# A two-layer transformer in float32: narrow matmuls in the feed-forwards, and a second copy of the last activations

## The reference

```python
def swiglu(x, w_gate, w_up, w_down):
    return (jax.nn.silu(x @ w_gate) * (x @ w_up)) @ w_down

for layer in range(2):
    ...
    h = h + 0.5 * swiglu(rms_norm(h, ffn1_norm_g[layer]), ffn1_w_gate[layer], ffn1_w_up[layer], ffn1_w_down[layer])
    ...  # layer 0: gated convolution, layer 1: attention; both with attention to a memory, then w_o
    h = h + 0.5 * swiglu(rms_norm(h, ffn2_norm_g[layer]), ffn2_w_gate[layer], ffn2_w_up[layer], ffn2_w_down[layer])
# second block: one normed input times w_in_2 (queries, keys, values, gates), a differential
# attention and an mLSTM attention, gated sums, w_out_2, norm, added to x
```

## Time and profile before

| | |
|---|---|
| time, median of 3 runs | 1188.84 us (1188.67 to 1189.12) |
| the profiled execution | 1188.1 us, span of the core 1186.5 us |
| TensorE busy | 1179.0 us, 99% of the span |
| VectorE busy | 862.4 us, 73% |
| ScalarE busy | 677.9 us, 57% |
| granted TensorE clock, mean | 0.999 |
| DMA | 215.85 MB, 182 GB/s |

### The profile page before, as it was taken

One profiled execution on the slowest core, in us unless ns is written; L12 is line 12 of the kernel. 1 busy time (PEld: TensorE's weight loads), 2 busy tenths in 40 slices (PEclk: granted clock), 3 DMA queues, 4 the chain that ended last, 5 costly groups with the idle time before them and its releaser, 6 DMA issues.

```text
span 1186.5 us, 18987 instructions
## 1 busy us (share of the span) xinstructions
PE 1179.0 (99%) x7592; PEld 1044.4 (88%) x7592; DVE 862.4 (73%) x1213; ACT 677.9 (57%) x1036; POOL 68.5 (6%) x86
## 2 busy tenths in 40 slices
PE   9999999999999999999999999999999999999998
PEld 8888889969988888888888888998888899879996
DVE  7977766896887767787766677677776668666875
ACT  7766644546665545655544557566554545566463
POOL 1601000200010000000000022000000000000000
PEclk9999999999999999999999999999999999999999
DMA  8855656564655555546555553255555565536440
GB/s 308 302 195 179 194 177 204 201 178 136 203 192 181 187 184 193 199 173 208 192 173 181 174 190 129 72 196 189 195 185 178 193 204 190 180 127 196 138 165 35
DMA packets 65398, 215.85 MB, mean 182 GB/s; under 512 B 8352, under 2 KB 12064, under 8 KB 65184
## 3 DMA queue, kind: packets, MB, share of 16 engines
q1 hardware_dynamic: 62608, 210.64, 53.0%
q10 hardware_dynamic: 2704, 4.02, 1.0%
HBM read 212.70 MB, written 1.93 MB: 181 GB/s over the span
## 4 chain that ended last, share of the span: by engine, by line
PE 95%; DVE 2%; ACT 1%; DMA 1%; issue 1%; POOL 0%; SPq 0%; ACTq 0%; DVEq 0%; POOLq 0%
PE psum L509 93%; DMA raw<-in_slots 1%; DVE wlo L1864 1%; ACT whi L1253 0%; PE psum L920 0%; DVE small L2308 0%; DVE oa L2516 0%; DVE acc L1926 0%; PE psum L1062 0%; PE psum L880 0%; PE psum L673 0%; PE psum L1203 0%; PE psum L970 0%; PE psum L1011 0%; POOL small L2739 0%
## 5 line engine op out<-in xcount | busy, mean ns | idle before, releaser
L509 PE MATMUL psum<-x,whi 128*128 128x512 f32 (+1 forms) x2512 | 633.0, 343 | 0.4 <-DVE aq L2451 0.3
L1864 DVE TENSOR_TENSOR wlo<-raw,whi 128x1024 fp32r<-128x1024 f32 (+2 forms) x402 | 474.6, 1192 | 166.0 <-ACT whi L1253 163.4
L1253 ACT CAST whi<-raw 128x1024 fp32r<-128x1024 f32 (+2 forms) x402 | 405.2, 1021 | 155.6 <-PE psum L509 146.7
L509 PE MATMUL psum<-x,wlo 128*128 128x256 f32 x1960 | 430.5, 279 | 0.0
L509 PEld LDWEIGHTS psum<-x,wlo 128*128 128x128 f32 x1960 | 366.8, 188 | 57.8
L509 PEld LDWEIGHTS psum<-x,whi 128*128 128x128 f32 x2512 | 382.1, 188 | 2.5 <-issue 0.9
L509 PE MATMUL psum<-g,whi 128*128 128x512 f32 x704 | 218.7, 392 | 0.0
L509 PEld LDWEIGHTS psum<-g,wlo 128*128 128x128 f32 x704 | 132.2, 188 | 29.5
L509 PE MATMUL psum<-whi,x 128*128 128x512 f32 (+1 forms) x512 | 140.6, 375 | 0.0
L509 PE MATMUL psum<-g,wlo 128*128 128x256 f32 x704 | 139.1, 279 | 0.0
L509 PEld LDWEIGHTS psum<-g,whi 128*128 128x128 f32 x704 | 106.8, 188 | 0.0
(11 more groups left out here) (317 smaller groups left out, 796.4 us busy)
## 6 DMA issues: line engine op xcount, KB each, us to landing
raw<-in_slots SPq DMA_DIRECT2D x371, 512.0 KB, 4.1
raw<-in_slots SPq DMA_DIRECT2D x16, 384.0 KB, 3.3
raw<-in_slots SPq DMA_DIRECT2D x16, 256.0 KB, 2.6
h<-conv_mem SPq DMA_DIRECT2D x8, 284.0 KB, 4.9
mkv<-in_mem ACTq DMA_DIRECT2D x1, 1024.0 KB, 11.2
memt<-in_mem_cols ACTq DMA_DIRECT2D x1, 1024.0 KB, 14.5
conv_mem<-hc SPq DMA_DIRECT2D x3, 288.0 KB, 2.3
h<-conv_mem SPq DMA_DIRECT2D x4, 142.0 KB, 2.9
```

Of the source, the lines that this page charges most:

```text
L509: return pe.matmul(o, l, r, start=start, stop=stop, skip_group_check=True)
L1253: act.copy(held(B.whi[:, i % SPLIT, :], *n), held(B.raw[:, i % RAW, :], *n)).then_inc(*s.hi.now(i))
L1864: dve.tensor_tensor(held(B.wlo[:, i % SPLIT, :], *n), held(B.raw[:, i % RAW, :], *n), held(B.whi[:, i % SPLIT, :], *n).bitcast(F32), ALU.s ...
```

## The change

- Up and gate sums of most column pairs are made narrow: pairs 2 to 6 in the first feed-forward, 2 to 4 and 6 to 10 in the second, 2 to 10 in the third and fourth (`NARROW_UP`). Narrow pairs alternate between banks 0 and 1 (gate) and 2 and 3 (up), and VectorE scales and multiplies straight from PSUM; copy and addition of halves go.
- All down sums are made narrow, also without halves.
- In the second to fourth feed-forward, in a wide pair that a narrow one follows, the last slot of up changes its order: its third and fourth block issue their four rounded matmuls, then their four rest matmuls (`last`).
- The last feed-forward's `prep` writes a second copy of the next activations, into `rh[1]`, `rl[1]` (`w2r`), and the rows of the last stage read that one.

```diff
+NARROW_UP = (tuple(range(2, 7)), (2, 3, 4, 6, 7, 8, 9, 10), tuple(range(2, 11)), tuple(range(2, 11)))
...
-            if late:
+            if late or (last and i >= 2):
                 two_rounded(b, h[:, k, :], x[:, kc], start and i == 0)
...
         if late:
             pe.wait_ge(*s.lo.at(slot))
-            for kc in ks:
+        if late or last:
+            for kc in ks if late else ks[2:]:
                 t = two_left(b, l[:, kc % 4, :], x[:, kc], stop and kc == ks[-1])
...
+    def read(done, part, f, p, narrow):
+        if p - 1 not in NARROW_UP[f]:
+            pe.wait_ge(*s.sum.at((part, f, p - 1)))
+        elif not narrow:
+            pe.wait_ge(*done.at((f, p - 1)))
+        elif p - 2 in NARROW_UP[f]:
+            pe.wait_ge(*done.at((f, p - 2)))
...
+            if narrow:
+                pair(xi, 0, up_slot(f, p), gate, range(4), True, False)
+                pair(xi, 0, up_slot(f, p) + 1, gate, range(4, 8), False, True)
+                read(s.mul, "up", f, p, narrow)
+                pair(xi, 0, up_slot(f, p) + 2, up, range(4), True, False)
+                pair(xi, 0, up_slot(f, p) + 3, up, range(4, 8), False, True)
+            elif p:
+                cols(x, 8, up_slot(f, p), gate)
+                read(s.mul, "up", f, p, narrow)
+                cols(x, 8, up_slot(f, p) + 2, up, last=f > 0 and p + 1 in NARROW_UP[f])
... (down)
-                t = two_blocks(b, h[:, k, :], l[:, k, :], F.g[:, kc], kc == 0, kc == 21, s.lo.at(i) if k == 0 else None)
+                for j in range(2):
+                    o, q = bank[b][:, j * S:(j + 1) * S], slice(j * 128, (j + 1) * 128)
+                    mm(o, h[:, k, q], F.gh[:, kc, :], kc + j == 0, False)
+                    mm(o, h[:, k, q], F.gl[:, kc, :], False, False)
+                    if k + j == 0:
+                        pe.wait_ge(*s.lo.at(i))
+                    t = mm(o, l[:, k, q], F.gh[:, kc, :], False, kc == 21)
... (second)
-        rows(X0, None, 8, VB2, 512, [[6], [7]])
+        rows(X1, "w2r", 8, VB2, 512, [[6], [7]])
... (ScalarE, ffn)
-            half(("down", f, p), down_slot(f, p) + 5, in_pairs(B.htmp[:, p % 2, :]), (4, 6, 0, 4)[p])
             prep(v, p, targets)
+            if f == 3:
+                for c in (2 * p, 2 * p + 1):
+                    act.activation(rh[1][:, c, :], hT[:, c, :], ACT.Copy, scale=gcol[:, c, 7:8]).then_inc(
+                        *s.x_hi.now(("w2r", c)))
```

More of the change, by code:

```diff
@@ L354, in signals @@
         for p in range(PAIRS):
-            sums += [("gate", f, p), ("up", f, p)]
-        sums += [("down", f, p) for p in P4]
+            if p not in NARROW_UP[f]:
+                sums += [("gate", f, p), ("up", f, p)]
     s.w = [sig(f"w_in{i}", range(i, SLOTS, RAW), 16) for i in range(RAW)]
@@ L545, in two_left, with part @@
         return t
-    def part(x, slot, b, ks, start, stop, gen=None, between=None):
+    def part(x, slot, b, ks, start, stop, gen=None, between=None, last=False):
         side(slot)
@@ L597, in pair, with cols @@
         t.then_inc(*s.used.now(slot))
-    def cols(x, K, slot, b, gen=None):
+    def cols(x, K, slot, b, gen=None, last=False):
         for i, k0 in enumerate(range(0, K, 4)):
-            part(x, slot + i, b, range(k0, min(K, k0 + 4)), k0 == 0, k0 + 4 >= K, gen)
+            part(x, slot + i, b, range(k0, min(K, k0 + 4)), k0 == 0, k0 + 4 >= K, gen, last=last and k0 + 4 >= K)
     def first_use(sig, gen, c):
@@ L703, in ffn @@
                 rows((rh[1], rl[1]), "mem0", 8, MKV0, 512, [[4], [5]])
+            narrow = p in NARROW_UP[f]
+            gate, up = (p % 2, 2 + p % 2) if narrow else (0, 2)
             if p:
-                pe.wait_ge(*s.sum.at(("gate", f, p - 1)))
+                read(s.gate, "gate", f, p, narrow)
             elif f == 1:
@@ L730, in ffn @@
             if p == 2:
-                pe.wait_ge(*s.sum.at(("gate", f, PAIRS - 1)))
+                read(s.gate, "gate", f, PAIRS, False)
             if p == 3:
@@ L1129, in second @@
         pe.wait_ge(*s.c_dve.at("gt"))
-        rows(X0, None, 8, VA2, 512, [[4], [5]])
+        rows(X1, None, 8, VA2, 512, [[4], [5]])
         rg = rest()
@@ L1416, in ffn @@
                     up_rounded(0)
-                if i == 0 and p:
+                if i == 0 and p and p - 1 not in NARROW_UP[f]:
                     up_half(p - 1)
@@ L1420, in ffn @@
                     up_rounded(p - 1)
-                if i == (2 if p else 1 if f == 0 else 3):
+                if i == (2 if p else 1 if f == 0 else 3) and p not in NARROW_UP[f]:
                     if p >= 2:
@@ L1433, in ffn @@
             for i in range(6):
-                if p == 0 and i == 0:
+                if p == 0 and i == 0 and PAIRS - 1 not in NARROW_UP[f]:
                     up_half(PAIRS - 1)
@@ L2012, in up_mul @@
             r, q = F.gr[:, p % 2, :], F.pr[:, p % 2, :]
+            u = q
+            if p in NARROW_UP[f]:
+                dve.wait_ge(*s.used.at(up_slot(f, p) + 3))
+                u = bank[2 + p % 2]
             dve.wait_ge(*s.silu.at((f, p)))
-            dve.tensor_tensor(q, r, q, ALU.mult).then_inc(*s.mul.now((f, p)))
+            dve.tensor_tensor(q, r, u, ALU.mult).then_inc(*s.mul.now((f, p)))
         def up_rest(p):
@@ L2059, in ffn @@
             pair = flat(hT[:, 2 * p:2 * p + 2, :])
-            halves(("down", f, p), tmp, (4, 6, 0, 4)[p])
-            dve.scalar_tensor_tensor(out=tmp, in0=tmp, scalar=0.5, in1=row, op0=ALU.mult, op1=ALU.mult).then_inc(
+            dve.wait_ge(*s.used.at(down_slot(f, p) + 5))
+            dve.scalar_tensor_tensor(out=tmp, in0=in_pairs(bank[(4, 6, 0, 4)[p]]), scalar=0.5, in1=row, op0=ALU.mult, op1=ALU.mult).then_inc(
                 *s.dve_step.tick())
@@ L2065, in ffn @@
             prep(v, p, targets)
+            if f == 3:
+                for c in (2 * p, 2 * p + 1):
+                    dve.wait_ge(*s.x_hi.at(("w2r", c)))
+                    dve.scalar_tensor_tensor(out=rl[1][:, c, :], in0=hT[:, c, :], scalar=gcol[:, c, 7:8],
+                                             in1=rh[1][:, c, :].bitcast(F32), op0=ALU.mult,
+                                             op1=ALU.subtract).then_inc(*s.x_lo.now(("w2r", c)))
     def add_h(v, p, slot, b, targets):
```

40 lines of the change are left out of this document (22 added, 18 removed).

## The result

| | before | changed |
|---|---|---|
| time, median | 1188.84 us (5 runs, 1188.40 to 1189.12) | 1199.11 us (5 runs, 1195.10 to 1201.24) |
| ratio | | 1.0082 (95% interval 1.0072 to 1.0093) |
| profiled execution | 1188.1 us | 1201.24 us |
| TensorE busy | 1179.0 us | 1192.6 us |
| VectorE busy | 862.4 us | 817.0 us |

Slower by 0.8%, forecast 1201.1 us. The page of the changed kernel (compare): VectorE and ScalarE got 45 and 41 us less to do, and the span grew by all that TensorE takes longer.

A forecast was written before the change was run, and what follows sets the result against it. TensorE, busy 99% of the span, bounds the kernel, so matmul density counts. Terms 12.4 + 0.9 + 0.3 (24 triples after the last feed-forward) - 1.3 = +12.3 us on 1188.84 give 1201.1 us; range 1182 to 1203.

The forecast's parts named there:

- The phase at the entries: Where wide blocks pass to narrow ones: all narrow stretches are entered slow and stay slow; chance 0.52, 1201.1 us.
- the step count: In the reordered slots: four rounded matmuls miss the fast place from either side, so four rest matmuls stand 0.118 us apart.
- a count modulo three: Each rounded matmul moves TensorE's phase one step of three; rest matmuls run fast in one place only.
- other places: Slots 2 and 3 show further starting places of the phase, so the rule was an inference from few rows.
- The price of a slow block: 760 up, gate and down blocks, narrow slow at 0.7063 us against wide 0.690: +12.4 us.
- The third feed-forward's down sums: 88 blocks on its unpadded g, taken at the slow value against 0.6965 us wide: +0.9 us, bounds -1.5 and +1.4.
- The last activations: Last stage's value and gate rows read the second copy, 0.680 us per group, not 0.701: -1.3 us, bounds -1.7 and 0.
- The waits and the halves at nothing: Dropped copy and addition of halves lie off the path; TensorE's new waits have some 5 us of cover: both 0.
- The comparison with a load of 107 ns: Skill's 128-column load is below 0.113 or 0.118 us between narrow matmuls, so no slow phase would exist; slow rows disagree.
- The first feed-forward's down sums: They start after an even count of blocks from a slow entry, so they come out slow too.

The follow-up runs named there:

- second experiment: Changed kernel with the reordered slot grouped otherwise: one block as it was, then six rounded and six rest matmuls; 1190.22 us (ratio 1.0010).
- plain entries: Changed kernel without the reordered slot, so twelve plain wide blocks stand in front of the narrow stretches; 1197.94 us (ratio 1.0082).
- odd-count kernel: Changed kernel with triples as last wide block before narrow stretches of the second to fourth feed-forward, replacing the reordered slot; 1188.99 us (ratio 1.0003).

## Why the prediction was right, and where it was off

**The phase at the entries, and the step count: right.** The first feed-forward's fourth block ended slow (29.99), the reordered slots ended slow from either side, and each narrow stretch kept its phase to its end. The step that carried the forecast was a count modulo three inferred from two runs of eight. It was thin evidence, and it is now borne out by runs of two, four, six and eight and by the distances that take turns. Only one of the two runs, the one at 9.87, follows from the count as stated; the other (15.82) needed the "other places" that the prediction named, and where such a run starts in the turn isn't explained.

**The price of a slow block: right.** Predicted 0.706 us against 0.690, measured 0.707. 760 x 0.0167 = 12.7 us for 12.4.

**The third feed-forward's down sums: undersized.** I took the slow value of other narrow blocks (0.706) and named 0.713 as the upper bound. Measured 0.712: 88 x (0.712 - 0.6965) = +1.4 us for +0.9. An excess like the one that g's place costs wide blocks comes on top of the slow narrow ones, and behind wide blocks it was larger still (0.720, in the run with the down sums alone).

**The last activations: about right.** From the first group of the value rows to the narrow blocks behind the last, in the trace of before and in that of the changed kernel:

```profile
1011.61 0.63 PE L509 MATMUL psum<-whi,x 128*128 128x512 f32 x2
...
1078.77 0.40 PE L509 MATMUL psum<-x,whi 128*128 128x256 f32 x2
```

```profile
1026.23 0.63 PE L513 MATMUL psum<-whi,x 128*128 128x512 f32 x2
...
1092.31 0.40 PE L513 MATMUL psum<-x,whi 128*128 128x256 f32 x2
```

67.16 us became 66.08: -1.1 us for -1.3.

**What was left out.** The output projection's blocks in mix_b lie behind transposes and changed their phase, though nothing in them was edited: fast in the trace of before, where 40 triples stand between the starts 762.25 and 775.85 (0.340 us each), slow in that of the changed kernel, 49 between 770.87 and 788.18 (0.353 us each). 56 x 0.0133 = +0.7 us. This isn't the change's doing: in the trace with the second copy alone, whose instructions are those of before up to there, they were slow too (0.353 us). With it the terms give 12.7 + 1.4 + 0.3 - 1.1 + 0.7 = +14.0 us, and the two profiled executions differ by 1201.24 - 1188.1 = 13.1. The remaining 0.9 us isn't assigned.

**The waits and the halves at nothing: right**, by the list of waits and by the run that keeps the halves.

**The comparison with a load of 107 ns.** The profile of the kernel before gives each load of 128 columns 188 ns, whichever the stretch, longer than the 0.113 us between fast narrow matmuls. So, as the profile draws them, loads overlap each other and the matmuls, and the length of a load doesn't tell a fast stretch from a slow one. What the loads have to do with the slow phase stays open.

**The scatter was not foreseen.** Five executions of the kernel before lie within 0.7 us (27 in the rounds of the first experiments within 2.5), five of the changed one within 6.1. The profiled one took 1201.24 us, so the forecast of 1201.1 fits it better than the median 1199.1; that fit is luck in part. The traces show a reason: of the seven with the same four wide blocks in front of the first narrow stretch four enter it slow, three fast. In the second experiment's trace it was fast:

```profile
30.21 0.39 PE L515 MATMUL psum<-x,wlo 128*128 128x256 f32 x2
```

One such entry is worth 80 x 0.027 = 2.1 us. The first feed-forward's down sums are worth 2.3 us; the prediction derived them slow from the count of blocks, as they were in the profiled execution, but in the runs with plain entries and with the halves, whose first feed-forward has the same matmuls in the same order and starts slow too, they were fast. In the odd-count kernel the fourth feed-forward would be worth 6.2 us, where mix_b leaves the other order. That kernel's ten times lie near 1185, 1190 and 1195.8 us, which fits these sizes; but only one of the ten has a trace, so it's an inference. Which entries differed in the other executions of the changed kernel can't be told either.

## What to carry to other kernels

When one engine is busy for 99% of the span, read the distance from start to start in each stretch, not the busy time or an instruction's duration: a stream can run at two speeds with no wait in sight, and the one it gets may be set many microseconds earlier. If so, find the rule on stretches that the present kernel already has, and choose what stands in front of each long stretch, or keep the form that averages over both speeds and hardly scatters. A change that wins in a stretch entered well can lose in all others.

## What the runs showed of the hardware

- Six matmuls of 256 columns for a block take 0.680 us or 0.707 us, four (two of 512, two of 256) 0.690 us on average, with the granted clock full in both. The faster value is the narrow form's, though it issues half as many instructions again.
- The phase moves with the wide form's 512-column matmuls, one step of three each, seen as distances of 226, 229 and 232 ns that take turns; 256-column triples keep it for 288 triples and more. Norm sums and transposes change it in narrow stretches in ways that differ from place to place and, in the first feed-forward and after mix_b, from execution to execution. Why isn't settled: no run here shows what inside the engine holds it.
- The place of an operand counts. At its old place g's wide blocks took 0.0065 us more each, and its slow narrow triples 0.356 us (0.360 behind wide blocks) and not 0.353; with a tile 80 bytes longer ahead of it the down sums turned slow behind fast triples (in two traces), with one 208 bytes longer they stayed fast (in one).
